# Output projection of the prompt tokens moved behind the last sample's attention; the sample tile routed first

## The chip, the cores and the metric

The kernel runs on one core of one Trainium2 chip. The number that counts is the device time of one launch in microseconds. Before the change it was 904.72 us (median of 3 runs, 903.98 to 906.97).

The engines run side by side and meet only at semaphores: TensorE (PE) for matmuls and transposes, VectorE (DVE), ScalarE (ACT), GpSimd (POOL), and SyncE (SP), which here only issues DMA transfers. All data is float32.

## The reference

One inference step of a decoder layer, for 272 prompt tokens (16 learned meta tokens and 256 real ones) and for 8 samples of 8 new tokens each. Each sample attends to 2048 cached tokens (16 pages of 128), in 8 heads of 64.

```
h   += W_out( sigmoid(gA) * P_A(RWKV(xn)) + sigmoid(gB) * P_B(attention(xn)) ),  xn = RMSNorm(h)
h   += MoE( RMSNorm(h) )          # 4 groups of 8 experts; best group, then its best 2 experts
y    = RMSNorm(h)                 # without the meta tokens
```

For a sample, attention runs over the pages of its cache and its own 8 tokens. The mixture (MoE) is routed by `x @ router`, 36 logits per token. In it each of the 32 experts has two 1024x256 matrices in and one 256x1024 out, so 3 MB, and every one of them is read: 96 MB and one expert's 3 MB more for a pass that takes the tokens beyond 32 per expert.

## The kernel before

The program is a row of blocks. All engines meet at the end of each. The change lies in the block `cache`, which starts near 420 us of the profile. Before it are the projections and the recurrent branch; behind it, from about 662 us, is the block `moe`.

In `cache` the loop over the samples b = 0 to 7 runs on TensorE as follows. `scores(b+1)` multiplies queries with the keys (matmul lines L1813, L1822, L1828, L1831). `turn_out(b-1)` transposes the finished output of the sample before (L1875), `turn_probs(b)` transposes the probabilities (L1845, L1848). `weigh(b)` multiplies them with the values (L1860, L1869). Then comes a helping of "fills".

A fill is a piece of the prompt tokens' projections, put between the steps of the samples so that TensorE has work while the samples' chain waits. There are 32, in the order of the list `kinds`: 8 of kind a (gated projection of the recurrent branch, 4 matmuls of 320 columns), 8 of kind b (the same for attention, 256 columns), both L1899, and 16 of kind o (output projection, 2 matmuls of 512 columns, L1890). The table `fill_no` says how many go where: `fills(n)` runs the fills from `fill_no[n]` up to `fill_no[n + 1]`. VectorE takes each result away in `fill_out`. Banks 5 and 6 of the accumulator serve both the fills and `turn_probs`.

After `weigh(7)` comes the tail. It has these steps:

- `sb` (L1943): kind b's projection for the 64 sample tokens; VectorE gates the result.
- `ho` (L1969): their output projection; VectorE adds it to h.
- For each of three tiles of tokens (0 and 1: 128 prompt tokens each, 2: the 64 sample tokens): the norm (`root` on ScalarE, `norm` on VectorE), `turn_x2` (L1929, transposes of the normed tile), `logits` (L1960).
- The choice of experts for all tiles at once, on VectorE (from L2212).

The samples' keys come in by DMA from SP (`key_loads(b)`, 16 pages of 256 KB, allowed once `scores(b-2)` is done). Their values are issued by GpSimd, sample b+1's quarter m once `weigh(b)` has used up quarter m. VectorE transposes the keys in place (`turn_keys`, L1497). In program order, it does the first half of sample b+2's keys before it may look at the scores of sample b+1. SP's queue is in order: a load that waits holds all that follow.

The weights of the experts go through 18 slots of 1 MB. SP loads them ahead (`ahead`), each as soon as its slot is no longer used by `cache`. From the 19th on, a load waits until `moe` has consumed what lies in its slot.

Of the kernel before, what the change touches and what calls it, by code (L numbers as in the profile page):

```python
# [13 lines left out]
DB, DS = 8, 8  # L14
# [81 lines left out]
def build(nc, A, O):  # L96
# [17 lines left out]
    with ctx:  # L114
# [1535 lines left out]
        gs_keep = rsT.rearrange("p b n -> p (b n)")[:, 0:ND * NS].rearrange("p (d t) -> p d t", d=ND)  # L1650
# [7 lines left out]

        tile_of = lambda a, i: a[:, 2 * i:2 * i + 2, :].rearrange("p a n -> p (a n)") if i < NT - 1 else a[:, NHT - 1, :]
# [23 lines left out]
        fill_no = [0, 2, 5, 8, 11, 14, 18, 24, 28, len(kinds)]  # L1683
# [28 lines left out]
        with nc.Block("cache") as block:  # L1712
            @block.sync
            def _(sp):
# [18 lines left out]
                proj_load(sp, 1, 0)  # L1733
                sp.wait_ge(S("fill_ps"), 4)
# [3 lines left out]
                key_loads(4)  # L1738
# [3 lines left out]
                key_loads(5)  # L1742
                key_loads(6)
# [27 lines left out]
                sp.wait_ge(S("ho_ps"), 1)  # L1771
                for s in (0, 1, 16, 10):
                    ahead(sp, s)

            @block.gpsimd
            def _(pool):
# [13 lines left out]
                pool.wait_ge(S("sco_ps"), DB)  # L1790
                nc.gpsimd.tensor_copy(gs_keep, gates[:, :, SEQ:TM]).then_inc(S("gs_kept"), 1)
# [12 lines left out]
            def _(pe):  # L1804
# [104 lines left out]
                for b in range(DB):  # L1909
# [5 lines left out]
                    if b == DB - 1:  # L1915
                        pe.wait_ge(S("pT_sb"), 4 * DB)
                        pe.wait_ge(S("pn_sb"), DB)
                        fills(DB)
                    weigh(b)
                    if b < DB - 1:  # L1920
                        fills(b + 1)
                tbank, lbank = (0, 5, 4), (0, 6, 4)

                def turn_x2(i):
                    pe.wait_ge(S("x2_ready"), i + 1)
# [12 lines left out]
                for h in range(2):  # L1938
                    pe.wait_ge(*proj_fill(1, h))
# [5 lines left out]
                mm.then_inc(S("sb_ps"), 1)  # L1945

                def pair_sums(name, b, col):
                    pe.wait_ge(S(name), NT)
# [3 lines left out]
                def logits(i):  # L1952
                    n = TROWS[i]
                    if i == 0:
                        pe.wait_ge(S("wr_in"), 16)
                    pe.wait_ge(S("x2T_a"), i + 1)
                    pe.wait_ge(S("x2T_b"), i + 1)
# [6 lines left out]
                logits(0)  # L1964
                pe.wait_ge(S("sb_sb"), 1)
                for k in range(KT):
# [4 lines left out]
                mm.then_inc(S("ho_ps"), 1)  # L1971
                logits(1)
                pe.wait_ge(S("rconst"), 1)
                pair_sums("ss2", 5, 0)
                turn_x2(2)
                logits(2)

# [739 lines left out]
```

## Time and profile before

| | us |
|---|---|
| median of 3 runs | 904.72 |
| the profiled execution | 901.19 |
| its span, first to last instruction | 899.6 |
| TensorE busy | 767.6 (85%) |
| VectorE busy | 374.3 (42%) |
| ScalarE busy | 186.5 (21%) |
| GpSimd busy | 149.6 (17%) |

The mean granted TensorE clock is 0.923 of full speed. The DMA engines moved 220.27 MB, 245 GB/s over the span. A time in the profile is counted from the span's start. An entry like `[11.80 <-issue]` says how long the engine was idle before the instruction and what ended that; "issue" means that the profile names no releaser.

### The profile page before, as it was taken

To read this page: it belongs to the slowest core of one execution; us is meant where nothing else is said; L and a number is where in the kernel's file an instruction comes from. 1 tells how busy PE (TensorE), PEld (TensorE's weight loads), DVE (VectorE), ACT (ScalarE), POOL (GpSimd) and SP (SyncE) were. 2 spreads that over 40 slices of the span, in tenths; PEclk is the share of its full clock that TensorE was granted. 3 is DMA by queue.
4 is the path that set the end of the run, shared out by engine and by line. 5 is a ranking of instruction groups with operands and counts; after the bars stand their busy time and mean duration, and the time that the engine had idled before them with its cause. 6 is when DMAs were issued, how large, how long until landed. Compare 5 with 4: busy or idle time off the path is not lost. (4 is left out here: it accounts for less than half of the span.)

```text
span 899.6 us, 20892 instructions
## 1 busy us (share of the span) xinstructions
PE 767.6 (85%) x8753; PEld 461.3 (51%) x8753; DVE 374.3 (42%) x683; ACT 186.5 (21%) x424; POOL 149.6 (17%) x300
## 2 busy tenths in 40 slices
PE   3999899998878979967887697989869997899985
PEld 2445566665566656743454565545744444444421
DVE  3022532338942235466872775724262222422213
ACT  3001222216331111012421322222111110111112
POOL 8400030007040020022043343333000000000000
PEclk9999899998978969968899799999969998999998
DMA  8533141122320212428899999987929999999993
GB/s 321 199 129 144 49 146 58 47 97 63 109 77 20 74 47 51 100 90 298 294 377 415 421 349 420 415 334 281 379 113 382 423 424 423 424 417 424 421 426 114
DMA packets 53239, 220.27 MB, mean 245 GB/s; under 512 B 21871, under 2 KB 24218, under 8 KB 28826
## 3 DMA queue, kind: packets, MB, share of 16 engines
q1 hardware_dynamic: 45456, 184.66, 53.2%
q0 software_dynamic: 7040, 34.10, 9.7%
q8 instruction: 69, 1.13, 0.5%
q10 hardware_dynamic: 650, 0.18, 0.1%
q14 instruction: 24, 0.20, 0.1%
HBM read 211.82 MB, written 7.09 MB: 243 GB/s over the span
## 5 line engine op out<-in xcount | busy, mean ns | idle before, releaser
L230 PE MATMUL bank<-arena 128*128 128x320 f32 x256 | 83.2, 468 | 3.5 <-PEq L112 3.5
L208 POOL DMA_DIRECT2D arena<-in_cv x112 | 59.2, 528 | 129.2 <-PE bank L1860 100.0
L530 PE MATMUL bank<-arena 128*128 128x336 f32 x224 | 70.9, 472 | 4.2 <-DVE arena L687 4.2
L2549 DVE TENSOR_TENSOR arena<-arena,bank 128x512 f32<-128x512 f32 x40 | 27.5, 687 | 106.9 <-PE bank L2337 103.8
L1497 DVE STREAM_TRANSPOSE arena<-arena 128x2048 f32<-128x2048 f32 x28 | 63.1, 2288 | 11.8 <-DMA arena<-in_ck 10.6
L2360 PE MATMUL bank<-arena 128*32 128x512 f32 x512 | 62.9, 596 | 2.7 <-DMA arena<-in_w_exp 2.0
L504 PE MATMUL bank<-arena 128*128 128x512 f32 (+1 forms) x144 | 62.3, 593 | 0.0
L230 PEld LDWEIGHTS bank<-arena 128*128 128x128 f32 x256 | 48.8, 201 | 24.7 <-issue 8.5
L530 PEld LDWEIGHTS bank<-arena 128*128 128x128 f32 x224 | 43.8, 200 | 27.2 <-issue 9.7
L1860 PE MATMUL bank<-arena 128*16 128x128 f32 x1024 | 36.2, 306 | 21.8 <-issue 19.1
L1315 ACT ACTIVATE arena<-bank 128x384 f32<-128x384 f32 (+6 forms) x63 | 26.0, 444 | 123.0 <-PE bank L230 46.2
L1860 PEld LDWEIGHTS bank<-arena 128*16 128x16 f32 x1024 | 32.9, 108 | 24.9 <-issue 20.6
L504 PEld LDWEIGHTS bank<-arena 128*128 128x128 f32 (+1 forms) x144 | 25.3, 177 | 35.3 <-issue 35.3
L1822 PE MATMUL bank<-arena 32*16 32x512 f32 x1024 | 40.8, 641 | 1.1 <-issue 1.1
L2465 ACT ACTIVATE arena<-bank 128x512 f32<-128x512 f32 x36 | 21.6, 599 | 94.3 <-PE bank L2328 59.9
L2016 ACT ACTIVATE arena<-bank 128x256 f32<-128x256 f32 x32 | 12.3, 385 | 124.6 <-PE bank L1845 123.7
L2391 PE MATMUL bank<-arena 128*32 128x512 f32 x256 | 31.2, 595 | 7.9 <-ACT arena L2505 5.7
L2360 PEld LDWEIGHTS bank<-arena 128*32 128x32 f32 x512 | 15.7, 109 | 43.3 <-issue 36.2
L2337 PE MATMUL bank<-arena 128*128 128x512 f32 x72 | 35.3, 617 | 1.4 <-ACT arena L2465 0.8
L2328 PE MATMUL bank<-arena 128*128 128x128 f32 x288 | 36.4, 287 | 0.0
L2328 PEld LDWEIGHTS bank<-arena 128*128 128x128 f32 x288 | 34.7, 201 | 1.3 <-issue 0.4
L1899 PE MATMUL bank<-arena 128*128 128x320 f32 (+1 forms) x128 | 32.9, 411 | 1.1 <-issue 1.1
(476 smaller groups left out, 1104.0 us busy)
## 6 DMA issues: line engine op xcount, KB each, us to landing
arena<-in_w_exp SPq DMA_DIRECT2D x99, 1024.0 KB, 20.0
arena<-in_ck SPq DMA_DIRECT2D x120, 256.0 KB, 7.0
arena<-in_cv POOLq DMA_DIRECT2D x112, 256.0 KB, 6.8
arena<-in_w_gate SPq DMA_DIRECT2D x8, 1024.0 KB, 4.8
arena<-in_w_za SPq DMA_DIRECT2D x7, 1024.0 KB, 6.8
arena<-in_w_zb SPq DMA_DIRECT2D x6, 1024.0 KB, 14.2
arena<-in_cv SPq DMA_DIRECT2D x16, 256.0 KB, 3.7
arena<-in_w_proj SPq DMA_DIRECT2D x8, 512.0 KB, 11.4
```

Of the source, the lines that this page charges most:

```text
L208: eng.dma_start(tile[n:P:4, :], src[bass.ds(page, 1)].rearrange("a (p j) n -> (a p) (j n)", j=4))\
L230: mm = nc.tensor.matmul(bank[b][:, 0:TM], w[:, k, a, :], xnT[:, k, NMETA:T], start=(k == 0), stop=(k == KT - 1))
L504: mm = nc.tensor.matmul(bank[q % 6][0:n, :], xnT[:, k, i * P:i * P + n], w[:, k % 4, :], start=(k == 0), stop=(k == KT - 1))
L530: mm = nc.tensor.matmul(bank[j % 2][:, 0:T], w[:, k, (j % 2) * P:(j % 2 + 1) * P], xnT[:, k, :], start=(k == 0), stop=(k == KT - 1))
L1497: return nc.vector.transpose(tile, tile)
L1822: mm = nc.tensor.matmul(bank[i][32 * g:32 * g + 2 * DS, :], qs[r, b, j, :], keys[b % 2][r, :, j, :], start=False, stop=(t == 3))
L1860: mm = nc.tensor.matmul(bank[7][32 * g:32 * g + 2 * DS, 0:P], pT[:, n, 2 * DS * g:2 * DS * (g + 1)], page_part(slot[4 + m], n % 4)[:, g * ...
L1899: mm = nc.tensor.matmul(out[:, 0:nt], w[:, d4, k, :], src[:, k, :], start=(k == 0), stop=(k == 3))
L2328: mm = nc.tensor.matmul(bank[half][:, k * P:(k + 1) * P], x2[:, 2 * i + half, k * P:(k + 1) * P], lhs_sel[:, i, :], start=False, stop=(k = ...
L2337: return nc.tensor.matmul(dst[:, :], gT[:, i, :], yg[:, half * HALF:(half + 1) * HALF], start=True, stop=True)
L2360: mm = nc.tensor.matmul(bank[2][j * CAP:(j + 1) * CAP, :], xg[:, q % 2, k, j * CAP:(j + 1) * CAP], place[s][:, (k % 4) * 512:(k % 4 + 1) * ...
L2391: mm = nc.tensor.matmul(bank[4 + half][j * CAP:(j + 1) * CAP, :], hT[:, f, j * CAP:(j + 1) * CAP], place[s][:, f * DM + half * 512:f * DM ...
```

## The change

`fill_no` gets 14 entries instead of 10. The loop now runs 2, 1, 2, 1, 2, 2, 2, 2 and, behind `weigh(7)`, 2 fills; these are all of kinds a and b. The 16 fills of kind o stand in the tail, four at a time: behind `sb`, behind `ho`, behind the sum of squares of the sample tile, and behind its transposes. Before, 12 of them were in the loop and 4 between `turn_probs(7)` and `weigh(7)`.

The sample tile goes through norm, transposes and logits first (`nth` gives each tile its place in the semaphores' counts); tiles 0 and 1 follow when the last fill is done. The banks of the tail change with it. The copy of the sample tokens' gates on GpSimd (`gs_keep`) goes; VectorE works in place.

On SP, the keys of sample 4 are loaded ahead of the second half of the b weights and of the prompt's rows, and those of samples 5 and 6 ahead of the gates for kind b, whose load waits for the eight a fills. ScalarE applies the sigmoid to these gates at sample 4 instead of 2. The last four loads of expert weights into slots that held `W_out` wait for all fills.

```diff
-        fill_no = [0, 2, 5, 8, 11, 14, 18, 24, 28, len(kinds)]
+        nth = lambda i: (i + 1) % NT + 1
+        fill_no = [0, 2, 3, 5, 6, 8, 10, 12, 14, 16, 20, 24, 28, len(kinds)]
@@ SP @@
                 proj_load(sp, 1, 0)
+                key_loads(4)
                 sp.wait_ge(S("fill_ps"), 4)
                 proj_load(sp, 1, 1)
                 for i in range(NT - 1):
                     sp.dma_start(tile_of(h2, i), A["xp"][i * P:(i + 1) * P, :]).then_inc(S("xr_in"), 16)
-                key_loads(4)
+                key_loads(5)
+                key_loads(6)
                 sp.wait_ge(S("fill_ps"), ND)
                 sp.wait_ge(S("fill_sb"), ND)
                 gates_load(1)
-                key_loads(5)
-                key_loads(6)
                 out_load(sp, 0)
...
                 sp.wait_ge(S("ho_ps"), 1)
+                sp.wait_ge(S("fill_ps"), NFILL)
                 for s in (0, 1, 16, 10):
                     ahead(sp, s)
@@ GpSimd @@
-                pool.wait_ge(S("sco_ps"), DB)
-                nc.gpsimd.tensor_copy(gs_keep, gates[:, :, SEQ:TM]).then_inc(S("gs_kept"), 1)
@@ TensorE @@
                     turn_probs(b)
-                    if b == DB - 1:
-                        pe.wait_ge(S("pT_sb"), 4 * DB)
-                        pe.wait_ge(S("pn_sb"), DB)
-                        fills(DB)
                     weigh(b)
-                    if b < DB - 1:
-                        fills(b + 1)
-                tbank, lbank = (0, 5, 4), (0, 6, 4)
+                    fills(b + 1)
+                tbank, lbank = (0, 2, 3), (0, 2, 4)
...
-                turn_x2(0)
                 turn_out(DB - 1)
-                turn_x2(1)
                 pe.wait_ge(S("ob_out"), DB)
...
                 mm.then_inc(S("sb_ps"), 1)
+                fills(DB + 1)
...
-                logits(0)
                 pe.wait_ge(S("sb_sb"), 1)
...
                 mm.then_inc(S("ho_ps"), 1)
-                logits(1)
+                fills(DB + 2)
                 pe.wait_ge(S("rconst"), 1)
-                pair_sums("ss2", 5, 0)
+                pair_sums("ss2", 1, 0)
+                fills(DB + 3)
                 turn_x2(2)
+                fills(DB + 4)
                 logits(2)
+                turn_x2(0)
+                turn_x2(1)
+                logits(0)
+                logits(1)
@@ ScalarE @@
-                    if b == 2:
+                    if b == 4:
                         gates_on(2)
...
+                act.wait_ge(S("att_ps"), DB)
+                act.wait_ge(S("h2_sb"), 2)
+                root(NT - 1)
+                turned(NT - 1)
                 for i in range(NT - 1):
                     act.wait_ge(S("fill_sb"), NFILL - 2 + 2 * i)
                     root(i)
-                act.wait_ge(S("gs_kept"), 1)
                 for i in range(NT - 1):
                     turned(i)
-                act.wait_ge(S("h2_sb"), 2)
-                root(NT - 1)
-                turned(NT - 1)
@@ VectorE @@
                 keep_out(DB - 2)
+                scale_out(DB - 1)
                 fills_out(DB)
+                keep_out(DB - 1)
...
-                norm(0)
-                norm(1)
-                scale_out(DB - 1)
-                keep_out(DB - 1)
-                dve.wait_ge(S("gs_kept"), 1)
-                for i in range(NT - 1):
-                    turned(i)
                 dve.wait_ge(S("sb_ps"), 1)
...
                 dve.sem_inc(S("sb_sb"), 1)
-                logits(0)
+                fills_out(DB + 1)
...
                     TT(h, bank[2 + n][:, 0:QTR], h, add).then_inc(S("h2_sb"), 1)
+                fills_out(DB + 2)
                 norm(NT - 1)
-                logits(1)
+                fills_out(DB + 3)
                 turned(NT - 1)
+                fills_out(DB + 4)
+                norm(0)
+                norm(1)
+                turned(0)
+                turned(1)
                 logits(NT - 1)
+                for i in range(NT - 1):
+                    logits(i)
```

TensorE's order from the last `turn_probs` to the choice of experts, in the kernel before (L1890 are o fills, L1860 and L1869 `weigh(7)`, L1929 transposes of the normed tiles, L1943 `sb`, L1969 `ho`, L1960 logits):

```order
L1848 MATMUL bank<-arena 8x64
L1890 MATMUL bank<-arena 128x512 x8
L1860 MATMUL bank<-arena 16x128 x64
L1869 MATMUL bank<-arena 16x128 x4
L1929 MATMUL bank<-arena 128x128 x8
L1875 MATMUL bank<-arena 128x64
L1929 MATMUL bank<-arena 128x128 x8
L1943 MATMUL bank<-arena 128x64 x32
L1960 MATMUL bank<-arena 128x36 x8
L1969 MATMUL bank<-arena 64x256 x32
L1960 MATMUL bank<-arena 128x36 x8
L1949 MATMUL bank<-arena 128x1
```

The same part of TensorE's program after the change, from `weigh(7)` on (L1859, L1868; L1898 b fills, L1933 `sb`, L1889 o fills, L1961 `ho`):

```order
L1859 MATMUL bank<-arena 16x128 x64
L1868 MATMUL bank<-arena 16x128 x4
L1898 MATMUL bank<-arena 128x256 x8
L1874 MATMUL bank<-arena 128x64
L1933 MATMUL bank<-arena 128x64 x32
L1889 MATMUL bank<-arena 128x512 x8
L1961 MATMUL bank<-arena 64x256 x32
L1889 MATMUL bank<-arena 128x512 x8
L1940 MATMUL bank<-arena 128x1
L1889 MATMUL bank<-arena 128x512 x8
L1923 MATMUL bank<-arena 128x128 x4
L1889 MATMUL bank<-arena 128x512 x8
```

Two b fills and all 16 o fills now stand behind `weigh(7)`, and the transposes and logits of the prompt tiles behind the last of them.

SP's order where the keys of sample 4 stand, before (L1507 is a half of the b weights, L1737 the prompt's rows, L208 a page of keys):

```order
L1507 DMA arena<-in_w_proj 128x2x512 x4
L1737 DMA arena<-in_xp 128x1024 x2
L1717 TENSOR_LOAD pt_row x4
L208 ISA
L208 DMA arena<-in_ck 32x2048
```

And after the change:

```order
L208 DMA arena<-in_ck 32x2048
L1507 DMA arena<-in_w_proj 128x2x512 x2
L1717 TENSOR_LOAD pt_row x4
L208 ISA
L208 DMA arena<-in_ck 32x2048
```

Two of the four weight transfers (1 MB) and both row transfers (1 MB) moved behind the 16 pages.

## Rows read from the trace of the kernel before

**Rows 1.** Chain of waits, stage of the experts: start, us, what.
```profile
671.56 7.07 PE bank L2360 x64
...
717.53 25.79 DMA arena<-in_w_exp
...
850.00 31.03 DMA arena<-in_w_exp
```

**Rows 2.** Stretches: busy time and count by engine, TensorE clock, DMA share, GB/s.
```profile
455.00:620.00 165.00, 134.63 (x2171) 87.33 (x2170) 91.17 (x134) 36.43 (x101) 61.40 (x126) 0.94 0.98 391
620.00:625.00 5.00, 5.00 (x80) 3.05 (x82) 2.59 (x6) 2.04 (x4) 0.00 (x0) 1.00 0.09 29
660.00:675.00 15.00, 11.61 (x87) 8.61 (x90) 8.57 (x29) 2.48 (x3) 0.00 (x0) 0.73 0.01 2
680.00:880.00 200.00, 179.55 (x1208) 79.46 (x1206) 48.58 (x90) 27.98 (x57) 0.00 (x0) 0.97 1.01 422
...
525.00:535.00 10.00, 10.00 (x153) 8.98 (x144) 6.24 (x9) 1.49 (x6) 5.03 (x10) 0.85 0.91 313
```

**Rows 3.** Timeline of VectorE: start, us, line, operation, [idle before <-releaser].
```profile
492.85 2.31 DVE L1497 STREAM_TRANSPOSE arena<-arena 128x2048 f32<-128x2048 f32 x1 [10.47 <-DMA arena<-in_ck]
...
626.42 1.28 DVE L2169 SCALAR_TENSOR_TENSOR arena<-arena 128x1024 f32<-128x1024 f32 x1
...
651.74 0.17 DVE L2212 TENSOR_REDUCE arena<-arena 128x3 f32<-128x12 f32 x1
```

**Rows 4.** Groups of TensorE by line: count, busy us, mean ns, idle before.
```profile
L1890 PE MATMUL bank<-arena 128*128 128x512 f32 x64 | 28.5, 597 | 1.6 <-DVEq L2119 1.2 <-ACT arena L2020 0.3
...
L1943 PE MATMUL bank<-arena 128*128 128x64 f32 x64 | 7.3, 274 | 0.0
...
L1969 PE MATMUL bank<-arena 128*64 128x256 f32 x64 | 7.1, 380 | 0.0
```

**Rows 5.** Timeline of TensorE, steps of the tail.
```profile
628.29 1.04 PE L1929 MATMUL bank<-arena 128*128 128x128 f32 x8
...
636.26 1.93 PE L1960 MATMUL bank<-arena 128*128 128x36 f32 x16
...
648.94 0.66 PE L1929 MATMUL bank<-arena 128*128 128x128 f32 x4 [1.53 <-DVE arena L2169]
```

**Rows 6.** Timeline of TensorE, the loop over samples.
```profile
502.05 6.36 PE L1860 MATMUL bank<-arena 128*16 128x128 f32 x128 [11.80 <-issue]
...
548.05 4.48 PE L1860 MATMUL bank<-arena 128*16 128x128 f32 x96 [1.97 <-issue]
...
554.82 3.72 PE L1899 MATMUL bank<-arena 128*128 128x256 f32 x16
...
573.81 3.90 PE L1860 MATMUL bank<-arena 128*16 128x128 f32 x128 [0.85 <-ACT arena L2016]
...
577.98 10.57 PE L1890 MATMUL bank<-arena 128*128 128x512 f32 x24
...
598.31 3.69 PE L1860 MATMUL bank<-arena 128*16 128x128 f32 x128 [1.37 <-issue]
...
616.05 7.10 PE L1890 MATMUL bank<-arena 128*128 128x512 f32 x16 [0.35 <-ACT arena L2020]
623.09 3.69 PE L1860 MATMUL bank<-arena 128*16 128x128 f32 x128
626.71 0.41 PE L1869 MATMUL bank<-arena 8*16 8x128 f32 x8
```

**Rows 7.** Timeline of ScalarE: the wait for the second gates.
```profile
503.39 2.34 ACT L1999 ACTIVATE arena<-arena 128x2560 f32<-128x2560 f32 x1 [11.59 <-DMA arena<-gates_dram]
```

**Rows 8.** Timeline of GpSimd: value pages of sample 5.
```profile
550.19 2.26 POOL L208 DMA_DIRECT2D arena<-in_cv  x4 [9.65 <-PE bank L1860]
...
563.50 0.52 POOL L1782 DMA_DIRECT2D arena<-out_v_s  x1
```

**Rows 9.** Value pages issued in 520 to 560 us, time to landing.
```profile
DMA to landing us min/median/max: 3.8/7.5/9.7
```

More of the change, by code:

```diff
@@ L1649, in build @@
         x2T = xnT[:, :, 0:TM]
-        gs_keep = rsT.rearrange("p b n -> p (b n)")[:, 0:ND * NS].rearrange("p (d t) -> p d t", d=ND)
         def turned_part(i, half, b):
@@ L1945, in _ @@
                 mm.then_inc(S("sb_ps"), 1)
+                fills(DB + 1)
                 def pair_sums(name, b, col):
-                    pe.wait_ge(S(name), NT)
+                    pe.wait_ge(S(name), 1)
                     nc.tensor.matmul(bank[b][:, col:col + 1], pair, ss[:, NT - 1:NT], start=True, stop=True)\
@@ L1962, in logits @@
                     mm.then_inc(S("lg_ps"), 1)
-                logits(0)
                 pe.wait_ge(S("sb_sb"), 1)
+                for c in range(4):
+                    pe.wait_ge(*out_fill(c))
                 for k in range(KT):
@@ L1971, in _ @@
                 mm.then_inc(S("ho_ps"), 1)
+                fills(DB + 2)
+                pe.wait_ge(S("rconst"), 1)
+                pair_sums("ss2", 1, 0)
+                fills(DB + 3)
+                turn_x2(2)
+                fills(DB + 4)
+                logits(2)
+                turn_x2(0)
+                turn_x2(1)
+                logits(0)
                 logits(1)
-                pe.wait_ge(S("rconst"), 1)
-                pair_sums("ss2", 5, 0)
-                turn_x2(2)
-                logits(2)
                 pe.wait_ge(S("pick_ready"), 1)
@@ L2172, in turned @@
                 def turned(i):
-                    dve.wait_ge(S("x2T_ps"), 2 * i + 1)
-                    nc.vector.tensor_copy(*turned_part(i, 0, (0, 5, 4)[i])).then_inc(S("x2T_a"), 1)
+                    dve.wait_ge(S("x2T_ps"), 2 * nth(i) - 1)
+                    nc.vector.tensor_copy(*turned_part(i, 0, (0, 2, 3)[i])).then_inc(S("x2T_a"), 1)
                 def logits(i):
-                    dve.wait_ge(S("lg_ps"), i + 1)
-                    ch(nc.vector.tensor_copy(lg[:, i, :], bank[(0, 6, 4)[i]][:, 0:E_]))
-                norm(0)
-                norm(1)
-                scale_out(DB - 1)
-                keep_out(DB - 1)
-                dve.wait_ge(S("gs_kept"), 1)
-                for i in range(NT - 1):
-                    turned(i)
+                    dve.wait_ge(S("lg_ps"), nth(i))
+                    ch(nc.vector.tensor_copy(lg[:, i, :], bank[(0, 2, 4)[i]][:, 0:E_]))
                 dve.wait_ge(S("sb_ps"), 1)
-                ch(TT(gs_keep, bank[4][:, :].rearrange("p (d t) -> p d t", d=ND), gs_keep, mult))
-                ch(TT(mT[:, :, SEQ:TM], mT[:, :, SEQ:TM], gs_keep, add))
+                gs_ = gates[:, :, SEQ:TM]
+                ch(TT(gs_, bank[4][:, :].rearrange("p (d t) -> p d t", d=ND), gs_, mult))
+                ch(TT(mT[:, :, SEQ:TM], mT[:, :, SEQ:TM], gs_, add))
                 dve.sem_inc(S("sb_sb"), 1)
-                logits(0)
+                fills_out(DB + 1)
                 dve.wait_ge(S("xs_in"), 32)
```

24 lines of the change are left out of this document (11 added, 13 removed).

## Prediction

> **What bounds the kernel now.** I read the chain of waits first. Its last third is the experts: TensorE starts the first expert matmuls at 671.56, and from then on the longest pieces are waits for expert weights, 25.79 us at 717.53 and 31.03 us at 850.00 [rows 1]. The stretches say the same: from 680 to 880 the DMA engines are fully busy at 422 GB/s, while in 660 to 675 they move 2 GB/s [rows 2]. So the weights that fit into the 18 free slots are there by 660, and the DMA engines then idle until the first experts free a slot. The other 81 MB-sized loads come after it, at a fixed rate. The end therefore lies a fixed time behind the start of the experts, and that start hangs on the choice of experts, which VectorE begins at 651.74 [rows 3]. I price the change by when this moment comes.
>
> Ahead of it are two stages with different limits. In the samples' loop, from 455 to 620, DMA is 0.98 busy at 391 GB/s, 64.5 MB in 165 us, against 422 in the last stage; behind it (620 to 625) it falls to 29 GB/s, so all that was asked for has landed by then. The weak place with a row of its own is 525 to 535, with 0.91 and 313 [rows 2]. In the tail, from the end of `weigh(7)` at 626.71 + 0.41 = 627.12 [rows 6] to 651.74, TensorE is the bound, and no key or value is waited for. The tail is 24.6 us.
>
> **What the change does to the tail.** The fills move out of a loop that DMA nearly fills, and into a tail that TensorE fills. Step by step from the end of `weigh(7)`:
>
> - Two b fills: 8 matmuls by name, 16 in the trace, 3.72 us [rows 6]. Then `turn_out` and the wait for VectorE's copy. In the kernel before, the two prompt tiles' transposes hide that; now I put 1.9 us. Together 5.6.
> - `sb` 7.3 and `ho` 7.1 [rows 4]: 14.4.
> - 16 o fills: all 64 matmuls of L1890 together are 28.5 us [rows 4]. VectorE's gating of `sb`, the add of `ho` and the norm of the sample tile lie under them, four fills (7.10 us, [rows 6]) at each place.
> - Transposes of the sample tile, 0.66 [rows 5]. Its logits fall into the wait for the prompt tiles' norms, so nothing. The pair sum is one column, nothing.
> - Behind the last fill: before, the last fill ended at 616.05 + 7.10 = 623.15 [rows 6] and the second prompt tile was normed at 626.42 + 1.28 = 627.70 [rows 3], 4.5 later. Then come its transposes, 1.04, a copy of about 0.7, logits of two tiles, 2 x 1.93 [rows 5], and a last copy, 0.2. Together 10.3.
>
> The sum is 5.6 + 14.4 + 28.5 + 0.7 + 10.3 = 59.5 us, against 24.6. The tail grows by 34.9 us. The bounds are narrow, since nearly all terms are rows: 33 if the wait for VectorE is nothing and copies overlap, 37 if each join costs half a microsecond. GpSimd's copy was off the path. The new wait of the last four expert loads for all fills is hidden: they are 4 MB, 10 us at 422 GB/s, and the fills are done 10 us before the choice begins, whose 20 us until the first expert matmul (651.74 to 671.56) come on top.
>
> **What the loop gives back.** The time of the moved fills is 28.5 + 3.7 = 32.2 us of TensorE. It comes back only where TensorE was the bound.
>
> Up to the weighing of sample 5 (573.81, [rows 6]) I take DMA for the bound. TensorE waits 11.80 us at 502.05 [rows 6] because VectorE stands 10.47 us before a key transpose [rows 3], and these are keys of sample 4. The change loads them 2 MB earlier, 5 us at 422 GB/s. But the transfers that they overtake, and the value pages asked for sooner, then arrive ahead of the next sample's keys. With full DMA engines a wait can only be handed on. What can be won is idle time: in 525 to 535 313 of 422 GB/s is 2.6 us, and I allow some more, because the value pages' requests come earlier and the loads that the loop needs go ahead of those that it doesn't. I take 6 us, between the bounds 0 and 16. The 16 is what eight fewer fills up to there (18 before, 10 now) would have saved a TensorE-bound loop, at about 2 us each. On the other side stands ScalarE: the gates for kind b are now asked for only after the eighth a fill, at sample 4, and ScalarE, which is in order, holds the exponentials of sample 5 until they land. Before, it stood 11.59 us there [rows 7], but at a place where TensorE was waiting anyway. I put this inside the range.
>
> From 573.81 to 627.12 it is 53.3 us before. TensorE ran through six fills (10.57), then 598.31 - (577.98 + 10.57) = 9.8 from the scores to the next weighing, and the four fills in front of `weigh(7)` [rows 6]. Now a period is 4.1 for the weighing, 3.7 for two b fills and 9.8 for the rest: 17.6 against 598.31 - 573.81 = 24.5, and I take 18.5. The last step is bound by the values: from the start of a weighing to the first page issued 550.19 - 548.05 = 2.1, to the last one 563.50 - 550.19 = 13.3 [rows 6, 8], 7.5 to 9.7 to land [rows 9], and 1.3 to use them. That is 24.2 to 26.4 from the start of `weigh(6)` to the end of `weigh(7)`, before 627.12 - 598.31 = 28.8. So the two together are 43.7 instead of 53.3: 9.6 won, with 5 to 12 as bounds.
>
> `weigh(7)` thus ends 6 + 9.6 = 15.6 us earlier, near 611.5, and the choice of experts begins at 611.5 + 59.5 = 671 instead of 651.7. The change costs 34.9 - 15.6 = 19.3 us. The profiled execution took 901.19 us (span 899.6), which would become 920.5. The median of the runs is 3.5 higher, so 904.7 + 19.3 = 924.
>
> One row speaks for a little more. Behind the 11.80 us wait the same 128 matmuls took 6.36 us, and 3.69 at full clock [rows 6]. In the new loop TensorE waits for DMA at more samples. The Trainium skill ("TensorE: Matmul & The Clock Gate", section "HAM oscillation — how this bites in real kernels") says that matmul bursts separated by waits for DMA each begin again at the low clock, which is a rule against taking filling work out of such a loop. The trace agrees at that place. By that rule the last two weighings would each lose 6.36 - 3.69 = 2.7 us, and the change would cost 24.7 us, so 929; the rows alone, where the waits of 1.37 and 0.85 us left the weighings at 3.69 and 3.90 us, leave it at 924.
>
> **Rivals.**
>
> 1. Faster: the loop was bound by TensorE. Its waits come from two key loads that were late by order, not by bandwidth; with the keys of sample 4 ahead, the 11.80 us go, and all of the 32.2 us of fills come back. The price is 34.9 - 32.2 - 11.8 = -9.1, so 896. It decides from the point where `weigh(7)` ends more than 35 us earlier, at 592 or before. For it: TensorE was busy 134.63 of 165 us. Against it: the 64.5 MB need 64.5 / 0.422 = 153 us, 12 less than they took, and even without the six expert loads and the small ones issued towards its end (about 6 MB, 14 us) that is 26 us less, not 35.
> 2. The keys do come earlier and the loop gains about 27 us, most of what DMA allows. Then 34.9 - 27 = 8, so 913.
> 3. The loop gains only what lies in front of `weigh(7)`: the stage up to sample 5 gives nothing, since ScalarE's wait for the gates moves onto the path, and the value pages take their slow landing. Then 5 is won, 30 lost: 934.
> 4. The change makes no difference because the expert weights hide the later start. For it: DMA is the bound of the last stage. Against it: in 660 to 675 nothing is left to load, and a later start only makes this hole longer. Together with a loop that gains just 35 this is the case of no change.
>
> **How the numbers follow.** The DMA-bound loop with 924 has 0.60; its own range is 916 to 931. Rival 2 has 0.15, rival 3 0.16, rival 1 0.05, no change 0.04. The range of 8 in 10 goes from 912 to 934. A measurement of this kernel tells about 0.3% from no change. Faster 0.05, within 0.3% 0.04, slower 0.91.
>
> **What would show it.** In the profile after: the end of `weigh(7)` (last L1868) near 611; behind it TensorE busy without a hole for some 50 us; the first L2212-like reduction of the choice near 671 and the first expert matmuls near 691; DMA at nearly nothing for over 30 us before them instead of 15; and the experts' stage of the same length, 228 us to the end of the span. In the loop, waits of TensorE at most samples and 0.98 or more DMA share. I am wrong if `weigh(7)` ends before 600, if the tail is shorter than 55 us, or if the experts' stage gets shorter when it starts later.

## The result and the profile after

The kernel after takes 933.78 us (median of 4 runs, 933.53 to 936.45), the kernel before 904.35 in the same comparison (4 runs, 899.84 to 906.97). The ratio is 1.033, with an interval of 1.029 to 1.036. The change costs 29.4 us where 19.3 were forecast. The profiled executions, 933.53 and 901.19 us, differ by 32.3, because that of before lies 3.2 us under its median. What follows is read from these two.

The chain of waits has the shape of [rows 1] and stands 30.6 us later:

```profile
702.18 7.08 PE bank L2362 x64
...
747.96 25.85 DMA arena<-in_w_exp
...
880.55 31.33 DMA arena<-in_w_exp
```

So the experts' stage is nearly what it was: 931.8 - 702.18 = 229.6 us to the end, before 228.0. The stretches: the first as in [rows 2], then a hole in which DMA idles and the last stage, both where they lie now, then the weak place:

```profile
455.00:620.00 165.00, 123.08 (x2242) 83.96 (x2242) 81.78 (x120) 36.51 (x101) 59.27 (x113) 0.85 1.02 411
642.00:666.00 24.00, 24.00 (x93) 11.72 (x88) 8.89 (x16) 2.11 (x5) 0.00 (x0) 1.00 0.00 1
704.00:904.00 200.00, 181.87 (x1267) 81.58 (x1260) 48.61 (x90) 27.59 (x56) 0.00 (x0) 0.98 1.00 416
525.00:535.00 10.00, 10.00 (x136) 5.70 (x138) 3.39 (x4) 0.00 (x0) 4.73 (x9) 0.80 1.02 424
```

DMA now moves 411 GB/s through the loop (before 391), and the weak place at 525 is gone (424, before 313). DMA now idles in two parts, from 642 to 668 us (1 GB/s) and from 680 to 704 (2 GB/s); between them come the expert loads that waited for the last fill. TensorE's clock in the loop fell from 0.94 to 0.85. In all, TensorE was busy 767.6 us before; the page of after has 20 us more, for the same number of instructions:

```profile
PE 787.8 (85%) x8753; PEld 473.0 (51%) x8753; DVE 374.2 (40%) x683; ACT 186.1 (20%) x424; POOL 148.8 (16%) x299
```

The loop on TensorE, to be held against [rows 6] (L1859 and L1868 are `weigh`, L1898 fills of kinds a and b):

```profile
495.93 6.49 PE L1859 MATMUL bank<-arena 128*16 128x128 f32 x128 [6.85 <-issue]
...
565.69 4.48 PE L1859 MATMUL bank<-arena 128*16 128x128 f32 x96 [3.97 <-issue]
572.00 1.07 PE L1859 MATMUL bank<-arena 128*16 128x128 f32 x32 [1.83 <-DMA arena<-in_cv]
...
573.34 5.41 PE L1898 MATMUL bank<-arena 128*128 128x256 f32 x16
...
588.52 3.69 PE L1859 MATMUL bank<-arena 128*16 128x128 f32 x128 [1.38 <-issue]
...
601.29 1.07 PE L1859 MATMUL bank<-arena 128*16 128x128 f32 x32 [1.91 <-DMA arena<-in_cv]
607.45 1.91 PE L1859 MATMUL bank<-arena 128*16 128x128 f32 x32 [5.09 <-DMA arena<-in_cv]
611.59 1.91 PE L1859 MATMUL bank<-arena 128*16 128x128 f32 x32 [2.23 <-DMA arena<-in_cv]
615.62 1.91 PE L1859 MATMUL bank<-arena 128*16 128x128 f32 x32 [2.12 <-DMA arena<-in_cv]
617.46 0.62 PE L1868 MATMUL bank<-arena 8*16 8x128 f32 x8
```

The 11.80 us wait of [rows 6] at the weighing of sample 2 is 6.85, and sample 5 is weighed from 565.69, 8.1 us earlier than before. Then it stops. Each quarter of `weigh(7)` waits for its value pages, 1.91 + 5.09 + 2.23 + 2.12 = 11.35 us, and three of the four run 1.91 us instead of 1.07. `weigh(7)` ends at 617.46 + 0.62 = 618.08, 9.0 earlier than before. GpSimd's first and last requests for the values of this sample, and the time of the 16 pages to landing:

```profile
590.25 2.26 POOL L208 DMA_DIRECT2D arena<-in_cv  x4 [9.25 <-PE bank L1859]
...
601.30 2.25 POOL L208 DMA_DIRECT2D arena<-in_cv  x4 [1.33 <-issue]
...
DMA to landing us min/median/max: 6.2/9.2/12.1
```

The same time for the last sample in the kernel before, whose pages were issued from 600 to 613 us:

```profile
DMA to landing us min/median/max: 6.5/7.9/9.6
```

The tail on TensorE, beside [rows 4, 5] (L1898 b fills, L1933 `sb`, L1961 `ho`, L1923 transposes of the second prompt tile, L1951 logits of both prompt tiles, L2330 matmuls of the first expert):

```profile
618.01 5.28 PE L1898 MATMUL bank<-arena 128*128 128x256 f32 x16
...
625.00 7.36 PE L1933 MATMUL bank<-arena 128*128 128x64 f32 x64 [1.54 <-DVEq L2092]
...
639.21 7.13 PE L1961 MATMUL bank<-arena 128*64 128x256 f32 x64
...
672.40 1.97 PE L1923 MATMUL bank<-arena 128*128 128x128 f32 x8 [0.78 <-DVE arena L2169]
674.16 6.88 PE L1951 MATMUL bank<-arena 128*128 128x36 f32 x32
...
695.82 5.67 PE L2330 MATMUL bank<-arena 128*128 128x128 f32 x32
```

It is full, as foreseen, but its ends run wholly or partly at half clock, granted 0.50 from 606 to 620 us and from 674 to 698: the two b fills take 5.28 us (3.72 in [rows 6]), the transposes of the second prompt tile 1.97 (1.04 in [rows 5]) and the 32 logit matmuls of the prompt tiles 6.88 (2 x 1.93 in [rows 5]). The choice, beside [rows 3]:

```profile
681.39 0.17 DVE L2214 TENSOR_REDUCE arena<-arena 128x3 f32<-128x12 f32 x1
```

The tail is 63.3 us long, before 24.6. Last, ScalarE's gates, beside [rows 7]: the wait is 1.10 instead of 11.59 us.

```profile
543.48 2.34 ACT L1997 ACTIVATE arena<-arena 128x2560 f32<-128x2560 f32 x1 [1.10 <-DMA arena<-gates_dram]
```

In sum: loop -9.0, tail +38.7, from the choice to the first expert matmul 20.8 instead of 19.8 (+1.0), experts' stage +1.6, together +32.3.

### The profile page after: what moved, and what is told of

It is laid out like the page before. It is cut to its first block and busy times, and to the rows that moved or that the text cites. A ratio compares the mean times of both kernels' runs of the same rounds, so it can differ in the third digit from the quotient of the medians.

```text
span 931.8 us, 20890 instructions
## 1 busy us (share of the span) xinstructions
PE 787.8 (85%) x8753; PEld 473.0 (51%) x8753; DVE 374.2 (40%) x683; ACT 186.1 (20%) x424; POOL 148.8 (16%) x299
## 5 line engine op out<-in xcount | busy, mean ns | idle before, releaser
L208 POOL DMA_DIRECT2D arena<-in_cv x112 | 59.1, 528 | 119.1 <-PE bank L1859 91.2
L1859 PE MATMUL bank<-arena 128*16 128x128 f32 x1024 | 42.1, 332 | 39.2 <-DMA arena<-in_cv 19.8
L1497 DVE STREAM_TRANSPOSE arena<-arena 128x2048 f32<-128x2048 f32 x28 | 63.5, 2293 | 12.6 <-DMA arena<-in_ck 11.5
L2362 PE MATMUL bank<-arena 128*32 128x512 f32 x512 | 63.2, 596 | 3.4 <-DMA arena<-in_w_exp 2.7
L504 PE MATMUL bank<-arena 128*128 128x512 f32 (+1 forms) x144 | 65.2, 615 | 0.0
L1859 PEld LDWEIGHTS bank<-arena 128*16 128x16 f32 x1024 | 34.5, 116 | 45.5 <-issue 22.4
L504 PEld LDWEIGHTS bank<-arena 128*128 128x128 f32 (+1 forms) x144 | 26.4, 184 | 37.1 <-issue 37.1
L2393 PE MATMUL bank<-arena 128*32 128x512 f32 x256 | 33.7, 624 | 7.2 <-ACT arena L2507 5.7
L1898 PE MATMUL bank<-arena 128*128 128x320 f32 (+1 forms) x128 | 39.5, 467 | 0.0
L2330 PE MATMUL bank<-arena 128*128 128x128 f32 x288 | 38.0, 295 | 0.0
L2330 PEld LDWEIGHTS bank<-arena 128*128 128x128 f32 x288 | 36.2, 208 | 1.3 <-issue 0.4
## 6 DMA issues: line engine op xcount, KB each, us to landing
arena<-in_w_exp SPq DMA_DIRECT2D x99, 1024.0 KB, 20.8
```

The lines of the kernel that those rows point to most:

```text
L208: eng.dma_start(tile[n:P:4, :], src[bass.ds(page, 1)].rearrange("a (p j) n -> (a p) (j n)", j=4))\
L504: mm = nc.tensor.matmul(bank[q % 6][0:n, :], xnT[:, k, i * P:i * P + n], w[:, k % 4, :], start=(k == 0), stop=(k == KT - 1))
L1497: return nc.vector.transpose(tile, tile)
L1859: mm = nc.tensor.matmul(bank[7][32 * g:32 * g + 2 * DS, 0:P], pT[:, n, 2 * DS * g:2 * DS * (g + 1)], page_part(slot[4 + m], n % 4)[:, g * ...
L1898: mm = nc.tensor.matmul(out[:, 0:nt], w[:, d4, k, :], src[:, k, :], start=(k == 0), stop=(k == 3))
L2330: mm = nc.tensor.matmul(bank[half][:, k * P:(k + 1) * P], x2[:, 2 * i + half, k * P:(k + 1) * P], lhs_sel[:, i, :], start=False, stop=(k = ...
```

## The experiments

Each kernel was timed beside the kernel before, whose median was 904.0, 902.5 and 905.75 us in the three comparisons; ratios are to it. Rows come from one profiled execution of each kernel. Executions of one kernel differ: 23 of the kernel before lay between 898.92 and 910.06 us. So a difference of 1 or 2 us between two traces says little.

**Expert loads held back.** On SP the six loads of expert weights issued in 560 to 586 us, ahead of the values of the last sample, wait for the end of `weigh(7)`; the small loads go first.

```diff
-                for s in (2, 3):
-                    ahead(sp, s)
...
-                for s in (11, 12, 13, 14):
-                    ahead(sp, s)
...
                 sp.dma_start(wr, A["w_r"]).then_inc(S("wr_in"), 16)
+                sp.wait_ge(S("pv_ps"), 4 * DB)
+                for s in (2, 3, 11, 12, 13, 14):
+                    ahead(sp, s)
```

> The changed kernel, with the six expert loads into the key slots held back until the last sample's values are used up; the small loads go first. Theory A (in the changed kernel the last sample's values land late, 12 us after their issue, because the expert loads share the DMA engines with them): the waits of 11.4 us inside the last weighing fall to 3 to 5 us, it ends 5 to 8 us sooner, near 611 in the profile, and the time is 926 to 929. The experts' stage is not longer, since the free slots are filled long before it. Theory B (the values are held up by their own queue, GpSimd's issue and landing): the last weighing ends at 618 as before and the time stays at 934 within 2.

Measured: 924.31 us (917.43 to 929.78), ratio 1.019 (1.012 to 1.026). Theory A holds for the waits in the last weighing (2.70 + 1.36 = 4.1 us) and for its end, 609.77 + 0.62 = 610.39; the median lies 1.7 us below its range. The value pages of the last sample, and TensorE from `weigh(6)` on:

```profile
DMA to landing us min/median/max: 3.3/3.7/5.4
```

```profile
589.00 3.69 PE L1858 MATMUL bank<-arena 128*16 128x128 f32 x128 [1.38 <-issue]
...
604.66 1.91 PE L1858 MATMUL bank<-arena 128*16 128x128 f32 x32 [2.70 <-DMA arena<-in_cv]
607.93 1.91 PE L1858 MATMUL bank<-arena 128*16 128x128 f32 x32 [1.36 <-DMA arena<-in_cv]
609.77 0.62 PE L1867 MATMUL bank<-arena 8*16 8x128 f32 x8
...
616.33 12.09 PE L1932 MATMUL bank<-arena 128*128 128x64 f32 x64 [1.53 <-DVEq L2091]
628.21 8.98 PE L1888 MATMUL bank<-arena 128*128 128x512 f32 x16
```

The pages land in 3.7 instead of 9.2 us. From the start of `weigh(6)` to the end of `weigh(7)` it is 610.39 - 589.00 = 21.4 us, in the kernel after 29.6; the forecast's bounds were 24.2 to 26.4, and its moment 611.5 is met. The whole loop, from the start of `weigh(0)`, is 160.3 us for 169.4. So most of what the last periods lose, they lose to SP's loads beside the value pages. The edit takes two kinds of them away at once: the 1 MB loads, and the small loads, which in the kernel after queue behind four of these, take 19 to 26 us to land and so run beside the last pages. Which of the two does it was not tested apart. In the profiled execution most of this is lost again at once: `sb` runs at half clock, 12.09 us for the 7.36 of after, and the four o fills behind it 8.98 for 7.08. The profiled execution took 929.78 us, at the upper end of the four; the median gains 9.5 us on the kernel after.

**Eight fills ahead of the last weighing.** Based on the kernel after; two b fills and six o fills cover the wait for values.

```diff
-        fill_no = [0, 2, 3, 5, 6, 8, 10, 12, 14, 16, 20, 24, 28, len(kinds)]
+        fill_no = [0, 2, 3, 5, 6, 8, 10, 12, 14, 22, 22, 26, 26, len(kinds)]
...
+                    if b == DB - 1:
+                        pe.wait_ge(S("pT_sb"), 4 * DB)
+                        pe.wait_ge(S("pn_sb"), DB)
+                        fills(DB)
                     weigh(b)
...
```

> The changed kernel, with the two b fills and six of the o fills put between the last sample's probabilities and its weighing. Theory A (from sample 5 on the end hangs on TensorE's work, and the last weighing's wait for values is a hole that the moved fills left open): the last weighing still ends near 618, the tail behind it is shorter by the eight fills, 14.3 us, and the time is 917 to 921. Theory B (a fill costs the same wherever it stands): the weighing ends 14 us later, the tail is 14 us shorter, 934 within 2.

Measured: 935.97 us (935.42 to 936.75), ratio 1.034 (1.029 to 1.039). Theory A missed. Theory B's number came, though not by its mechanism: the weighing ends at 623.07 + 0.41 = 623.48, 5.4 us later and not 14. The fills did cover the wait: `weigh(7)` ran through in 3.69 us. But the tail behind it ran at half clock for longer:

```profile
619.45 3.69 PE L1859 MATMUL bank<-arena 128*16 128x128 f32 x128
...
624.95 13.48 PE L1938 MATMUL bank<-arena 128*128 128x64 f32 x64 [0.56 <-DVEq L2097]
639.99 10.04 PE L1966 MATMUL bank<-arena 128*64 128x256 f32 x64 [1.56 <-DVEq L2189]
```

`sb` took 13.48, `ho` 10.04 us, both at half clock or nearly; with eight fills fewer, the tail was still 685.46 - 623.48 = 62.0 us long, 1.3 less than in the kernel after.

**Keys of sample 4 early, alone.** The kernel before with one call of its SP program moved.

```diff
                 proj_load(sp, 1, 0)
+                key_loads(4)
                 sp.wait_ge(S("fill_ps"), 4)
...
-                key_loads(4)
                 sp.wait_ge(S("fill_ps"), ND)
```

> The kernel before, with the one edit that the keys of sample 4 are loaded ahead of the second half of the b weights and the prompt's rows. Theory A (the loop up to sample 5 is bound by DMA traffic): the wait of 11.8 us at sample 2 shrinks to about 7, but later waits grow; the weighing of sample 5 moves by less than 3 us, and the time is 902 to 906. Theory B (the order of the loads was the fault): the stage ends 8 to 12 us sooner, 893 to 897.

Measured: 911.36 us (907.82 to 915.08), ratio 1.008 (1.005 to 1.010): slower than both theories had it.

```profile
516.75 3.78 PE L1899 MATMUL bank<-arena 128*128 128x256 f32 x8 [15.21 <-DVEq L2117]
```

```profile
508.65 2.34 ACT L1999 ACTIVATE arena<-arena 128x2560 f32<-128x2560 f32 x1 [15.21 <-DMA arena<-gates_dram]
```

The 11.80 us wait at the weighing of sample 2 is gone (1.97 is left). In its place ScalarE stands 15.21 us for the gates, for 11.59 in [rows 7], VectorE cannot empty the fills' banks, and TensorE waits 15.21 us in front of a fill. The gates' wait was there before, beside the other one. The kernel after applies the gates at sample 4, where ScalarE waits 1.10 us for them; what that is worth has no term of its own in the forecast.

**Tail order alone.** The kernel after with the loop, the loads and the fills of before; only the order of the tail is new.

```diff
-        fill_no = [0, 2, 3, 5, 6, 8, 10, 12, 14, 16, 20, 24, 28, len(kinds)]
+        fill_no = [0, 2, 5, 8, 11, 14, 18, 24, 28, 32, 32, 32, 32, len(kinds)]
...
-                key_loads(5)
-                key_loads(6)
+                key_loads(4)
                 sp.wait_ge(S("fill_ps"), ND)
                 sp.wait_ge(S("fill_sb"), ND)
                 gates_load(1)
+                key_loads(5)
+                key_loads(6)
...
-                    if b == 4:
+                    if b == 2:
                         gates_on(2)
```

> The loop, the fills and the loads of the kernel before, with the changed kernel's order of the tail (sample tile first, prompt tiles routed behind it). Theory A (the loss is the moved fills; the new order only opens the waits that the prompt tiles' steps used to cover): the tail is 3 to 8 us longer than 24.6, the time 908 to 912. Theory B (routing the sample tile first carries a good part of the loss by itself): 915 or more. Theory C (the order is free): 905 within 2.

Measured: 919.69 us (916.30 to 923.41), ratio 1.016 (1.010 to 1.022), so some 15 us, as theory B had it. Lines L1938 `sb`, L1966 `ho`, L1928 and L1956 transposes and logits:

```profile
629.56 11.99 PE L1938 MATMUL bank<-arena 128*128 128x64 f32 x64 [0.56 <-DVEq L2097]
643.12 9.91 PE L1966 MATMUL bank<-arena 128*64 128x256 f32 x64 [1.57 <-DVEq L2189]
...
661.39 3.85 PE L1928 MATMUL bank<-arena 128*128 128x128 f32 x16 [1.01 <-DVE arena L2174]
665.03 4.05 PE L1956 MATMUL bank<-arena 128*128 128x36 f32 x32
```

The tail is 669.42 - 628.10 = 41.3 us, 16.7 longer. Before, the prompt tiles' transposes and logits stood between the steps of the sample tile and covered VectorE; now there are waits of 0.47, 0.56, 1.57, 1.86, 1.52, 0.56 and 1.01 us, 7.6 in all, and `sb` and `ho`, behind the first three of them, run 11.99 and 9.91 us instead of 7.26 and 7.13. In the kernel after the moved fills cover most of this: there the tail without its 32.2 us of fills is 31.1, 6.5 more than before, where the forecast had 2.7.

**Half of the key bytes, before and after.** Half the width of every key page is loaded from sample 2 on. The other half of these keys is left out, 12.6 MB in all.

```diff
-                            page_load(sp, place[s], n, A["ck"], pages[n], full[s])
+                            sp.dma_start(place[s][n:P:4, 0:SLOT // 2],
+                                         A["ck"][bass.ds(pages[n], 1)].rearrange("a (p j) n -> (a p) (j n)", j=4)
+                                         [:, 0:SLOT // 2]).then_inc(full[s], 16)
```

> The kernel before, with only half the width of every key page loaded (1 MB instead of 2... that is 128 KB of each page's 256 KB; the other half of the slot keeps what lay there). It leaves out half of the key bytes, 16 MB over the samples, some 12 MB of them in the loop, 28 us of DMA at 422 GB/s. Theory A (the loop is bound by DMA): the waits for keys go and the value pages land sooner; the loop ends 8 to 20 us earlier, 884 to 896. Theory B (the loop is bound by TensorE and the chain through VectorE and ScalarE): 900 to 905. It is the partner of the next kernel; what counts is the difference of the two.

> The kernel after, with the same half of the key bytes left out. Theory A (the moved fills could not be paid back because DMA, not TensorE, bounded the loop): now TensorE bounds it, so the fills taken out of it shorten it by 24 to 32 us instead of 9, and the difference between after and before shrinks from 29 us to between 5 and 16. Theory B (the loop gives nothing back because its waits are of the samples' chain and of order, whatever the bytes): the difference stays at 26 to 32 us.

Measured: 894.47 us (890.49 to 897.25), ratio 0.990 (0.987 to 0.994), and 919.38 us (914.25 to 925.77), ratio 1.018 (1.014 to 1.023). Theory A holds for the kernel before. The difference of the two is 24.9 us, between what the two theories had. The rows tell why. With all bytes, the loop from the start of `weigh(0)` to the end of `weigh(7)` is 179.4 us before and 169.4 after, 10.0 less. With half the key bytes it is, in their traces, 621.40 - 447.89 = 173.5 us for the kernel before and 598.03 + 0.62 - 449.27 = 149.4 for the kernel after, 24.1 less:

```profile
449.27 3.69 PE L1861 MATMUL bank<-arena 128*16 128x128 f32 x128 [0.16 <-ACT arena L2016]
...
598.03 0.62 PE L1870 MATMUL bank<-arena 8*16 8x128 f32 x8
...
605.27 11.47 PE L1935 MATMUL bank<-arena 128*128 128x64 f32 x64 [1.54 <-DVEq L2094]
616.53 9.63 PE L1891 MATMUL bank<-arena 128*128 128x512 f32 x16
```

The kernel before gains 5.9 us of loop from the missing bytes, the kernel after 20.0. So DMA did hold the loop of the kernel after: with the bytes gone, the moved fills are paid back at 24 of 32 us. Of these 14 us more, 6 are lost in the tail, to `sb` and the fills behind it at half clock again. The profiled executions differ by 22.2 us, the medians by 24.9.

**Gates one sample later.** The kernel before with the keys of sample 4 early and the gates out of their way.

```diff
-        fill_no = [0, 2, 5, 8, 11, 14, 18, 24, 28, len(kinds)]
+        fill_no = [0, 2, 5, 8, 8, 12, 18, 24, 28, len(kinds)]
...
+                key_loads(4)
                 sp.wait_ge(S("fill_ps"), 4)
...
-                    if b == 2:
+                    if b == 3:
```

> The kernel before with the keys of sample 4 loaded ahead of the second half of the b weights and the prompt's rows, ScalarE's gates one sample later (3 instead of 2), and the fills of that period put off to later ones (2, 3, 3, 0, 4, 6, 6, 4, 4). The earlier keys alone gave 911, with a TensorE wait of 15.21 us for banks that VectorE could not empty without the gates. Theory A (what a wait loses in this loop is handed on as long as DMA is 0.97 busy): the 11.80 us wait goes, but later keys and values are late instead; 898 to 905. Theory B (the wait is one of order): 10 us are won, 890 to 896.

Measured: 908.18 us (907.05 to 909.25), ratio 1.006 (1.003 to 1.008), above both theories. The wait moved on by one sample, for the keys of sample 5:

```profile
524.68 5.22 PE L1860 MATMUL bank<-arena 128*16 128x128 f32 x128 [15.59 <-issue]
```

**2 MB less in front.** The last kernel with two loads behind the keys of sample 5.

```diff
-                sp.wait_ge(S("fill_ps"), 4)
-                proj_load(sp, 1, 1)
-                for i in range(NT - 1):
-                    sp.dma_start(tile_of(h2, i), A["xp"][i * P:(i + 1) * P, :]).then_inc(S("xr_in"), 16)
...
                 key_loads(5)
+                sp.wait_ge(S("fill_ps"), ND)
+                proj_load(sp, 1, 1)
+                for i in range(NT - 1):
+                    sp.dma_start(tile_of(h2, i), A["xp"][i * P:(i + 1) * P, :]).then_inc(S("xr_in"), 16)
                 key_loads(6)
```

> The kernel c4_gates_at_3 (908) with the second half of the b weights and the prompt's rows, 2 MB that nothing uses before 553 us, loaded behind the keys of sample 5 instead of ahead of the gates. In c4 TensorE waited 15.59 us before the weighing of sample 3, for keys of sample 5, which stood behind these 2 MB and 1.25 MB of gates. Theory A (bytes in front of the late keys): 2 MB are 5 us at 422 GB/s, the wait shrinks to about 11, and the kernel comes to 902 to 905, level with before. Theory B (order alone bounds): the wait goes to 2 us and it is 893 to 898. Theory C (handed on to the keys of sample 6): 906 to 910.

Measured: 905.17 us (900.47 to 909.69), ratio 0.999 (0.996 to 1.003), level with the kernel before. The wait for the keys of sample 5 shrank from 15.59 to 3.28 us, more than the 2 MB are worth, and one of 9.07 us stood up at sample 4:

```profile
515.06 5.53 PE L1860 MATMUL bank<-arena 128*16 128x128 f32 x128 [3.28 <-issue]
...
546.16 5.71 PE L1860 MATMUL bank<-arena 128*16 128x128 f32 x128 [9.07 <-issue]
```

**The prompt's rows late, alone.** The kernel before.

```diff
-                for i in range(NT - 1):
-                    sp.dma_start(tile_of(h2, i), A["xp"][i * P:(i + 1) * P, :]).then_inc(S("xr_in"), 16)
                 key_loads(4)
...
                 key_loads(6)
+                for i in range(NT - 1):
+                    sp.dma_start(tile_of(h2, i), A["xp"][i * P:(i + 1) * P, :]).then_inc(S("xr_in"), 16)
```

> The kernel before with one change: the prompt's rows (1 MB, first used near 563 us) are loaded behind the keys of sample 6 instead of ahead of those of sample 4. The keys of sample 4, and the gates behind them, come 2.4 us earlier, and nothing that is used earlier comes later. Theory A (the 11.80 us wait at the weighing of sample 2 is one for bytes in front): 2 to 2.5 us are won there and kept, 900.5 to 902. Theory B (handed on): 902.5 to 904.5, no difference.

Measured: 903.00 us (898.33 to 905.79), ratio 0.997 (0.994 to 1.000). It is the only whole kernel below the one before, by 2.7 us, and the interval just touches no difference. In the profile the wait of 11.80 us is 9.76 and a new one of 4.70 stands before the weighing of sample 5; the loop is 178.8 us for 179.4. A gain is likely, but not shown.

**Two fills ahead of each weighing.** The kernel before; TensorE's short waits for the copies of the probabilities get cover.

```diff
-                    if b == DB - 1:
-                        pe.wait_ge(S("pT_sb"), 4 * DB)
-                        pe.wait_ge(S("pn_sb"), DB)
-                        fills(DB)
+                    pe.wait_ge(S("pT_sb"), 4 * b + 4)
+                    pe.wait_ge(S("pn_sb"), b + 1)
+                    early = fill_no[b + 1] + 2 if b < DB - 1 else fill_no[DB + 1]
+                    for f in range(fill_no[b + 1], early):
+                        fill(f)
                     weigh(b)
```

> The kernel before with two of each sample's fills put between its turn_probs and its weigh, where TensorE waits 1.4 to 2.0 us for the copies of the probabilities; nothing is moved to another sample. Theory A (DMA-bound loop): the weighing starts 1.5 to 3 us later in each sample, so the value pages of the next are asked for later too, and nothing is won: 902 to 910. Theory B (TensorE-bound loop): 1.5 us in each of six samples is won, 893 to 898.

Measured: 909.70 us (903.33 to 911.65), ratio 1.007 (1.004 to 1.010): nothing is won, as theory A had it. The short waits went, and others came: 2.74 us twice in front of the third fill, whose bank VectorE had not emptied, and 3.13 for values at sample 4.

**Keys of sample 4 late in the kernel after.**

```diff
-                key_loads(4)
                 sp.wait_ge(S("fill_ps"), 4)
...
+                key_loads(4)
                 key_loads(5)
```

> The kernel after with one thing undone: the keys of sample 4 are again loaded behind the second half of the b weights and the prompt's rows, right ahead of those of samples 5 and 6. Theory A (what an earlier load gains at one sample is handed on, since DMA is full and the last weighing waits for values anyway): the wait at the weighing of sample 2 grows from 6.85 us to 11 to 13, but the loop ends within 2 us of where it did; 932 to 937. Theory B (the earlier keys are what the loop gave back, the forecast's 6 us): 938 to 942.

Measured: 936.91 us (931.19 to 940.17), ratio 1.036 (1.030 to 1.043), 3 us above the kernel after but with overlapping intervals. The median lies in theory A's range, and the wait at sample 2 grew to 13.20 us, as theory A had it. But the loop, from the start of `weigh(0)`, is 621.38 - 446.04 = 175.3 us, 5.9 longer than in the kernel after, and that is theory B. The medians do not settle it: in this execution, the fastest of the four, the logits of the prompt tiles ran 4.09 instead of 6.88 us and paid half of it back.

**turn_out ahead of the b fills**, on top of the held expert loads.

```diff
                     weigh(b)
+                    if b == DB - 1:
+                        turn_out(b)
                     fills(b + 1)
...
                 scale_out(DB - 1)
+                keep_out(DB - 1)
                 fills_out(DB)
-                keep_out(DB - 1)
```

> The kernel of e1_hold_experts (924) with turn_out of the last sample moved between weigh(7) and the two b fills, and VectorE's copy of it ahead of their gating; the two fills then cover the copy for which TensorE waited 1.53 us before sb. In e1 sb ran 12.09 us behind this wait, and 7.36 in the kernel after. Theory A (the wait in front of sb costs the high clock): sb takes 7.3 us and the four o fills behind it 7.1 instead of 8.98, so with the wait 7 to 8 us are won: 915 to 919. Theory B (the clock falls there because of the waits in the last weighing, whatever stands before sb): only the wait goes, 921 to 926.

Measured: 922.47 us (917.25 to 923.70), ratio 1.017 (1.011 to 1.024).

```profile
616.55 7.25 PE L1932 MATMUL bank<-arena 128*128 128x64 f32 x64
623.64 7.08 PE L1888 MATMUL bank<-arena 128*128 128x512 f32 x16
...
665.61 6.88 PE L1950 MATMUL bank<-arena 128*128 128x36 f32 x32
```

The profile is as theory A had it: no wait before `sb`, 7.25 us for it and 7.08 for the fills, and a span of 921.7 for 927.8. The median lies in theory B's range, only 1.8 us below that of the kernel with held loads (924.31, from 917 to 930). A likely reason is that `sb` does not run at half clock in every execution there; only one of them was profiled, so this stays open.

## Why the prediction was wrong

- **What bounds the kernel, and the shift of the experts' stage: right.** The stage is 229.6 us for 228.0, and the hole in front of it grew from some 15 us to 26 and 24, where I had over 30.
- **The number.** 933.8 us lies at the upper end of the range from 912 to 934, and above the 916 to 931 of the mechanism that was held likeliest.
- **The loop up to the weighing of sample 5: right**, 8.1 us for the 6 forecast, within wide bounds, and 9.1 if counted from the start of `weigh(0)`. By the trace of the kernel with late keys 4.9 of these come from the earlier keys, though the medians do not show that. Of four kernels with earlier keys or fewer bytes ahead of them (keys of sample 4 early, gates one sample later, 2 MB less in front, the rows late) none was clearly faster: each time another wait took the place of the shortened one. The half keys show that bytes are behind it.
- **The failed step: "So the two together are 43.7 instead of 53.3: 9.6 won".** It was 618.08 - 565.69 = 52.4, so 0.9 won. The way to add it up was right, its terms were mis-sized. The period of sample 5 is 22.8 us for 18.5: the weighing with its wait for values takes 7.7 for 4.1, the two fills 5.4 for 3.7. The last one is 29.6 for 25.2. To the first request it is 1.7 us and from there to the last 13.3, as forecast; but the last pages need 12.1 to land, where I took 7.5 to 9.7 [rows 9], and 2.5 to be used at half clock, where I took 1.3. With SP's loads held the two periods are 610.39 - 569.28 = 41.1 us.
- **Why the landing was mis-sized stays open in part.** SP's loads make it long: 3.7 us without them. But the kernel before had the same four 1 MB loads and the same small ones beside the last sample's pages, and these landed in 7.9 us, at most 9.6, inside what I took. In the kernel after the pages of samples 4 to 6 are slow too, 8.9 to 9.3 us at the median and 11.5 to 12.2 at most, in a loop that moves 411 GB/s for 391. Part of it may be the single execution: the kernel with `turn_out` ahead, whose program is the same up to there, landed the pages of samples 4 and 5 in 7.9 and 7.3 us.
- **The tail: +38.7 for +34.9.** The steps and their order were right. What was missing is the half clock: 5.28 - 3.72 = 1.6 us in the b fills, 1.97 - 1.04 = 0.9 in the transposes, 6.88 - 3.86 = 3.0 in the logits, together 5.5; the other terms came out 1.7 us lower than forecast.
- **The clock.** With 1.7 us more in the fills at 573.34, 1.0 in the first expert's L2330 (5.67 for 4.71) and 1.0 behind the last wait of `weigh(7)` (its other slow quarters are followed by a wait for values, which hides them), the half clock is about 9.2 us of the 13.0 by which the profiled executions differ more than forecast. The Trainium skill ("TensorE: Matmul & The Clock Gate", section "HAM oscillation — how this bites in real kernels") says that matmul bursts parted by DMA waits start over at the low clock. I set that aside, since waits of 0.85 and 1.37 us had left the weighings at full clock [rows 6]. The trace agrees with the rule: behind the waits of 5.09, 2.23 and 2.12 us 32 matmuls took 1.91 us, and 1.07 at full clock. By that rule alone I had 929, but by losses in the last two weighings: the first of them ran in 3.69 us, at full clock, and most of the loss fell on the fills and the tail, which the forecast had at full clock.
- **The rivals.** The number, 934, is that of the third, and so is half of the mechanism: the slow landing. That the numbers meet is chance: it had 5 us won and 30 lost, the traces have 9.0 won, and 38.7 + 1.0 + 1.6 lost. Its other half, that the stage up to sample 5 gives nothing because of the gates, did not come (1.10 us of wait). The first, a loop bound by TensorE, fails by its own sign, since `weigh(7)` ends at 618 and not by 592; with half the key bytes gone 24.1 of the 32.2 us come back, with all bytes 10.0.
- **The order of the tail**, which I charged with 2.7 us, costs some 15 alone. In the kernel after the fills lie over most of it. So it looks cheaper beside the moved fills than it is.

Open: what makes the value pages land later than before; how often `sb` falls to half clock in unprofiled executions, and why `sb` kept the full clock in the kernel after, behind the same 1.54 us wait.

## What to carry to other kernels

Work that covers a chain's waits is not free to move just because the stage that it leaves is bound by something else: count what it covered, and look at the clock of what runs beside the new waits. When the end of a stage hangs on a landing time, put a wide range on it, and ask what can be held back from beside it: the same 256 KB pages took 3.7 us, 7.9 or 9.2 at the median here, and only the first of these has a reason that was shown. In a loop whose DMA engines are 0.98 busy, expect a wait that is removed by order alone to come back: here another wait took its place in each of four kernels, and the only gain among them, 2.7 us, was not clear of noise.

## What the runs showed of the hardware

- 256 KB pages of GpSimd's queue landed in 3.7 us at the median when SP's 1 MB loads were held and its small loads ran first. With four 1 MB loads issued ahead of them, and small ones behind those, it was 9.2 us in the kernel after and 7.9 in the kernel before. The small loads (128 to 512 KB) landed in 19 to 26 us behind the four, and in 5 to 6 ahead of them.
- TensorE fell to its lower level (1.2 of 2.4 GHz) with no wait for DMA nearby: with tail order alone it was granted 1.00 from 600 to 630 us, busy 25.3 of the 30; behind `weigh(7)` and idle gaps of 0.47 and 0.56 us, its clock was 0.50 from 634 to 646, and 64 matmuls of 64 columns took 11.99 us instead of 7.26.
